# Two feed-forward networks of a hybrid block on one core: pairs of feature tiles by seven half-size products in place of eight

## What is computed

```python
def swiglu(u, w_gate, w_up, w_down):
    return (jax.nn.silu(u @ w_gate) * (u @ w_up)) @ w_down
# u: (528 or 512 tokens, 1024); w_gate, w_up: (1024, 2816); w_down: (2816, 1024)
h = h + 0.5 * swiglu(rmsnorm_2(h, gain), w_gate, w_up, w_down)
```

## Times and profile before

| | us |
|---|---|
| median of three runs (1994.71 to 1995.18) | 1994.72 |
| span of the profiled execution | 1993.0 |
| TensorE busy | 1977.9 |
| GpSimd busy | 939.8 |
| VectorE busy | 870.8 |
| ScalarE busy | 743.8 |

### The profile page before, as it was taken

The page is one execution under the profiler, slowest core; times in us unless marked ns, Lnnn a source line. Parts: engine busy times, 40 slices in busy tenths (PEclk is TensorE's granted clock), DMA queues, the critical chain, the costliest instruction groups (busy, mean ns, idle before and its releaser), DMA issues.

```text
span 1993.0 us, 30195 instructions
## 1 busy us (share of the span) xinstructions
PE 1977.9 (99%) x11350; PEld 1694.2 (85%) x11350; DVE 870.8 (44%) x1516; ACT 743.8 (37%) x1132; POOL 939.8 (47%) x1220
## 2 busy tenths in 40 slices
PE   9999999999999999999999999999999999999998
PEld 6788777899999998789998888888888888888887
DVE  7854776722222225985442253433343542222212
ACT  5733555522222225534443252423334332222321
POOL 6432211654445555453333445354545665554554
PEclk9999999999999999999999999999999999999999
DMA  5211101222222333222111313122322222222322
GB/s 198 78 64 54 43 33 33 85 95 95 90 89 92 99 98 104 74 96 74 64 64 52 115 64 99 66 91 74 101 74 83 93 89 95 95 95 95 104 99 83
DMA packets 49882, 168.68 MB, mean 85 GB/s; under 512 B 6400, under 2 KB 8576, under 8 KB 49792
## 3 DMA queue, kind: packets, MB, share of 16 engines
q1 hardware_dynamic: 46864, 161.89, 24.4%
q10 hardware_dynamic: 2928, 5.51, 0.8%
HBM read 165.29 MB, written 2.10 MB: 84 GB/s over the span
## 4 chain that ended last, share of the span: by engine, by line
PE 94%; DVE 4%; ACT 1%; issue 0%; DMA 0%; DVEq 0%; ACTq 0%
PE slot L2133 93%; DVE qkv L1475 1%; DVE x_lo L1897 0%; PE slot L2588 0%; DVE xt L1889 0%; PE slot L2318 0%; DVE qkv L1472 0%; PE slot L2283 0%; DVE slot L1469 0%; DMA small<-small_in 0%; ACT mixed_hi L966 0%; DVE xt L1428 0%; PE slot L2586 0%; ACT rs L881 0%; DVE x_lo L1435 0%
## 5 line engine op out<-in xcount | busy, mean ns | idle before, releaser
L2666 POOL TENSOR_TENSOR w_lo<-w_raw,w_hi 128x256 fp32r<-128x256 f32 x1216 | 939.6, 805 | 1043.0 <-ACT w_hi L844 784.3
L2133 PE MATMUL slot<-x_hi,w_hi 128*128 128x264 f32 (+1 forms) x1864 | 640.7, 344 | 0.9 <-DVE x_lo L1897 0.7
L2133 PE MATMUL slot<-x_hi,w_lo 128*128 128x264 f32 (+1 forms) x1864 | 629.2, 338 | 0.0
L2133 PE MATMUL slot<-x_lo,w_hi 128*128 128x264 f32 (+1 forms) x1864 | 627.6, 337 | 0.0
L2133 PEld LDWEIGHTS slot<-x_hi,w_hi 128*128 128x128 f32 x1864 | 350.7, 188 | 48.2 <-issue 7.6
L2133 PEld LDWEIGHTS slot<-x_hi,w_lo 128*128 128x128 f32 x1864 | 350.8, 188 | 38.1 <-issue 1.4
L2133 PEld LDWEIGHTS slot<-x_lo,w_hi 128*128 128x128 f32 x1864 | 350.0, 188 | 38.8
L844 ACT ACTIVATE w_hi<-w_raw 128x1024 fp32r<-128x1024 f32 x215 | 225.4, 1054 | 313.8 <-PE slot L2133 305.8
L2133 PE MATMUL slot<-f_hi,w_hi 128*128 128x264 f32 (+2 forms) x550 | 173.5, 316 | 0.0
L2133 PE MATMUL slot<-f_hi,w_lo 128*128 128x264 f32 (+2 forms) x550 | 173.3, 315 | 0.0
L2133 PE MATMUL slot<-f_lo,w_hi 128*128 128x264 f32 (+2 forms) x550 | 172.9, 314 | 0.0
(11 more groups left out here) (366 smaller groups left out, 2863.5 us busy)
## 6 DMA issues: line engine op xcount, KB each, us to landing
w_raw<-weights SPq DMA_DIRECT2D x303, 512.0 KB, 3.2
h<-x_t ACTq DMA_DIRECT2D x4, 512.0 KB, 6.3
dec<-decays ACTq DMA_DIRECT2D x4, 264.0 KB, 3.1
const<-consts SPq DMA_DIRECT2D x1, 576.0 KB, 6.4
at_rot<-rotations ACTq DMA_DIRECT2D x1, 528.0 KB, 4.7
ix_rot<-rotations ACTq DMA_DIRECT2D x1, 528.0 KB, 6.7
rt_rot<-rotations ACTq DMA_DIRECT2D x1, 528.0 KB, 3.8
w_raw<-weights SPq DMA_DIRECT2D x2, 256.0 KB, 4.2
```

The lines of the kernel that those rows point to most:

```text
L2133: return nc.tensor.matmul(out, lhsT, rhs, start=start, stop=stop)
L2666: nc.gpsimd.tensor_tensor(w_lo[j][:, piece], w_raw[j][:, piece], w_hi[j][:, piece].bitcast(F32), ALU.subtract).then_inc(s_lo, 1)
```

## The change

The two feature tiles of a job and the two halves of the tokens make a 2 x 2 block product. It is done by Strassen's scheme in Winograd's form: seven products of 128 x (4 x 128) blocks by half the columns. With A11 to A22 the weight blocks (input tiles are taken in pairs, so `turned` reorders the stream: even tiles, then odd) and B11 to B22 the token blocks, the stationary operands are A11, S1 = A21 + A22, S2 = S1 - A11, A12, S3 = A11 - A21, S4 = A12 - S2 and A22; the moving ones are B11, B12 and B21 (together "B2"), B22, T1 = B12 - B11, T3 = B22 - B12, T2 = T3 + B11 and T4 = B21 - T2.

Each operand has its own high and low part, single-buffered, in places of 512 columns: VectorE makes the four sums of a job one job ahead (`sums`), ScalarE rounds each of the seven when the product of the job before has used its place (`operand_high`), GpSimd makes the low part in one instruction of 512 columns (`operand_low`). The products accumulate in four half-used banks (`pa`, `pe`, `pb`, `pc`; two sets, alternating by job). P2 goes on top of P1; `pb` is seeded by ScalarE with P1 and takes P6, then P3; `pc` is seeded with `pb` and takes P7, then P4. VectorE adds the rest (`evac_job`).

`down` has the same form over rounds of 4 pairs of inner tiles: after gate pairs 4 and 8 come four jobs each that add a round to `h`. The last 6 inner tiles are done as before at the end, for each model tile one weight block and 6 x 3 matmuls (twice that in network 1). The last model tile in network 2 has two column parts still, of 18 matmuls each. In the stages before the networks, `add_to_h` makes the T operands too (`x_parts`) and, at tile 4, the first job's sums. The loops of the engines are written out in place of the hardware loops.

```diff
+def ffn_jobs():
+    jobs = []
+    for p in range(KF // 2):
+        jobs.append(("gate", p))
+        if p and p % ROUND == 0:
+            jobs += [("down", p // ROUND - 1, d) for d in range(KD // 2)]
+        jobs.append(("up", p))
+    return jobs
+ROUND = 4
+ROUNDS = KF // 2 // ROUND
+REST = KF - 2 * ROUND * ROUNDS
+JOBS = ffn_jobs()
+PRODUCTS = ["P1", "P5", "P6", "P2", "P7", "P3", "P4"]
+OPERANDS = ["A11", "S1", "S2", "A12", "S3", "S4", "A22"]
+SUMS = ["S1", "S3", "S2", "S4"]
+BANKS = ["pa", "pe", "pb", "pc"]
+X_PARTS = ["B11", "T1", "T2", "B2", "T3", "T4"]
+X_MADE = ["B11", "T1", "B2", "T3", "T2", "T4"]
+F_PARTS = ["B11", "B2", "T"]
+OPS_OF_FFN = len(X_PARTS) * KD // 2 + len(F_PARTS) * ROUND * ROUNDS + REST
...
+def operand_place(i, name):
+    o = OPERANDS.index(name)
+    return (FFN_FIRST[i] + o // 2) % RING, slice(o % 2 * 512, o % 2 * 512 + 512)
...
+                    sp.wait_ge(s_flo, operand_at(i, n, "A22" if second else "A12"))
+                    sp.wait_ge(s_sum, sum_at(i, n, "S4"))
+                sp.dma_start(w_raw[j][:], w_dram[b // RING, j]).then_inc(s_raw[j], 16)
...
+            def operand_high(i, n, name):
+                j, cols = operand_place(i, name)
+                if n:
+                    act.wait_ge(s_prod, product_at(i, n - 1, PRODUCTS[OPERANDS.index(name)]))
+                else:
+                    act.wait_ge(s_used, whole(FFN_FIRST[i] - RING) + OPERANDS.index(name) // 2 + 1)
+                if name in SUMS:
+                    act.wait_ge(s_sum, sum_at(i, n, name))
+                else:
+                    wait_raw(act, FFN_FIRST[i] + 2 * n + (name[1] == "2"))
+                nc.scalar.activation(w_hi[j][:, cols], weight_part(i, n, name), ACT.Copy).then_inc(s_fhi, 1)
...
+                for n, (kind, p) in enumerate((job[0], job[1]) for job in JOBS):
+                    before = JOBS[n - 1] if n else ("", 0)
+                    nxt = n + 1 < len(JOBS)
+                    if n:
+                        operand_high(i, n, "A22")
+                    else:
+                        operand_high(i, 0, "A22")
+                    for taken in FREE["pb", i, n]:
+                        wait_evac(act, taken)
+                    copy_on(slot(("pb", i, n))[:, 0:half], "pa", "P1", n, 3 * job_at(i, n))
+                    if n == 0:
+                        token_parts(i, KD - 1, width, ("T2", "B2"))
+                    if nxt:
+                        operand_high(i, n + 1, "A11")
+                    act.wait_ge(s_prod, product_at(i, n, "P5"))
+                    if n:
+                        wait_evac(act, ("pb", i, n - 1))
+                    nc.scalar.activation(p5[:, 0:half], slot(("pe", i, n))[:, 0:half], ACT.Copy).then_inc(evac_at(("pe", i, n))[0], 1)
+                    if n == 0:
+                        token_parts(i, KD - 1, width, ("T3", "T4"))
+                        if i == 1:
+                            residual_square(KD - 1)
+                    if nxt:
+                        operand_high(i, n + 1, "S1")
+                    if before[0] == "gate":
+                        for j in range(2):
+                            act.wait_ge(s_q, gates(i, before[1]) + j + 1)
+                            nc.scalar.activation(square[j][:, 0:width], square[j][:, 0:width], ACT.Silu).then_inc(s_fsilu, 1)
+                    for taken in FREE["pc", i, n]:
+                        wait_evac(act, taken)
+                    copy_on(slot(("pc", i, n))[:, 0:half], "pb", "P6", n, 3 * job_at(i, n))
+                    if nxt:
+                        operand_high(i, n + 1, "S2")
+                        operand_high(i, n + 1, "A12")
+                    if before[0] == "up":
+                        ffn_parts(i, before[1], width, ("B11", "B2", 0, 1))
+                    copy_on(u3[:, 0:half], "pc", "P7", n, 3 * job_at(i, n))
+                    if before[0] == "up":
+                        ffn_parts(i, before[1], width, ("T",))
+                    if n == 0:
+                        rsqrt(("norm", 2 * i - 1), 1.0 / D, width)
+                        made["table"] = None
+                    if nxt:
+                        operand_high(i, n + 1, "S3")
+                        operand_high(i, n + 1, "S4")
...
+            def sums(i, n):
+                b = FFN_FIRST[i] + 2 * n
+                wait_raw(dve, b)
+                wait_raw(dve, b + 1)
+                part = lambda name: weight_part(i, n, name)
+                for name, x, y, op in (("S1", "A21", "A22", ALU.add), ("S3", "A11", "A21", ALU.subtract),
+                                       ("S2", "S1", "A11", ALU.subtract), ("S4", "A12", "S2", ALU.subtract)):
+                    if job_at(i, n):
+                        dve.wait_ge(s_flo, len(OPERANDS) * (job_at(i, n) - 1) + OPERANDS.index(name) + 1)
+                    if name in ("S2", "S4"):
+                        dve.wait_ge(s_sum, sum_at(i, n, "S1" if name == "S2" else "S2"))
+                    V.sig(nc.vector.tensor_tensor(part(name), part(x), part(y), op), s_sum, sum_at(i, n, name))
...
+                x_parts(i, j, w)
+                if j == 4:
+                    sums(i, 0)
...
+                def ffn_product(p):
                     for j in range(2):
...
+                        dve.wait_ge(s_fsilu, (i - 1) * KF + 2 * p + j + 1)
+                        V.sig(nc.vector.tensor_tensor(xt[j][:, 0:width], xt[j][:, 0:width], square[j][:, 0:width], ALU.mult),
+                              s_opraw, f_part(i, p, j if p >= ROUND * ROUNDS else F_PARTS[j]))
+                    if p >= ROUND * ROUNDS:
+                        return
+                    raw = fo_raw[:, p % ROUND, :, 0:half]
+                    b11, b12 = xt[0][:, 0:half], xt[0][:, half:width]
+                    b21, b22 = xt[1][:, 0:half], xt[1][:, half:width]
+                    V.sync()
+                    V.own(nc.vector.tensor_tensor(raw[:, 3], b12, b11, ALU.subtract))
+                    V.own(nc.vector.tensor_tensor(raw[:, 5], b22, b12, ALU.subtract))
+                    V.sync()
+                    V.own(nc.vector.tensor_tensor(raw[:, 4], raw[:, 5], b11, ALU.add))
+                    V.sync()
+                    V.sig(nc.vector.tensor_tensor(raw[:, 6], b21, raw[:, 4], ALU.subtract), s_opraw, f_part(i, p, "T"))
+                def ffn_low(p):
+                    if p >= ROUND * ROUNDS:
+                        for j in range(2):
+                            f = 2 * (p - ROUND * ROUNDS) + j
+                            part_low(f_lo[:, f, 0:width], xt[j][:, 0:width], f_hi[:, f, 0:width], f_part(i, p, j))
+                        return
+                    hi, lo = (x[:, p % ROUND, :, 0:half] for x in (fo_hi, fo_lo))
+                    part_low(lo[:, 0], xt[0][:, 0:half], hi[:, 0], f_part(i, p, "B11"))
+                    part_low(lo[:, 1:3], halves(xt[1][:, 0:width]), hi[:, 1:3], f_part(i, p, "B2"))
...
+                def evac_job(n, kind, d, late):
+                    pa, pb, pc = ((bank, i, n) for bank in ("pa", "pb", "pc"))
+                    ps = lambda key: slot(key)[:, 0:half]
+                    if kind == "down":
+                        o11, o12, o21, o22 = (h[:, 2 * d + a, c0 + c * half:c0 + c * half + half] for a in range(2) for c in range(2))
+                        t12, t22 = (x[:, 0:half] for x in xt)
+                    else:
+                        dst = square if kind == "gate" else xt
+                        o11, o12, o21, o22 = (dst[a][:, c * half:c * half + half] for a in range(2) for c in range(2))
+                        t12, t22 = o12, o22
+                    n1, n2 = norm[:, 0:half], norm[:, half:width]
+                    def final(ins_out, src, scale):
+                        if kind == "down":
+                            return nc.vector.scalar_tensor_tensor(ins_out, src, 0.5, ins_out, ALU.mult, ALU.add)
+                        return nc.vector.tensor_tensor(ins_out, src, scale, ALU.mult)
+                    dve.wait_ge(s_prod, product_at(i, n, "P2"))
+                    V.sig(final(o11, ps(pa), n1), *evac_at(pa))
+                    dve.wait_ge(s_seed, 3 * job_at(i, n) + 3)
+                    V.own(nc.vector.tensor_tensor(t22, u3[:, 0:half], p5[:, 0:half], ALU.add))
+                    V.sync()
+                    V.own(final(o22, t22, n2))
+                    late()
+                    dve.wait_ge(s_prod, product_at(i, n, "P3"))
+                    V.sig(nc.vector.tensor_tensor(t12, ps(pb), p5[:, 0:half], ALU.add), *evac_at(pb))
+                    V.sync()
+                    if kind == "gate":
+                        V.sig(final(o12, t12, n2), s_q, (i - 1) * KF + 2 * d + 1)
+                    else:
+                        V.own(final(o12, t12, n2))
+                    dve.wait_ge(s_prod, product_at(i, n, "P4"))
+                    V.sig(final(o21, ps(pc), n1), *evac_at(pc))
+                    V.sync()
+                    if kind == "gate":
+                        dve.sem_inc(s_q, 1)
```

(74 more changed lines are left out.)

412 lines of the change are left out of this document (229 added, 183 removed).

## The result

The changed kernel takes 2136.49 us (median of four runs, 2135.5 to 2140.44) beside 1994.72 of the kernel before on the same chip: a ratio of 1.0714, 95% interval 1.0699 to 1.0729. The change costs 142 us. The forecast was +80, in a range up to 2140. So the direction was right and the size some 60 us short. The profiled execution has a span of 2135.4 us, against 1993.0.

What follows compares the result with a forecast made beforehand. The prediction took TensorE to bound the kernel before and time shared by VectorE and GpSimd the changed one: 1993 + 67 (networks) + 14 (edges) = 2074, plus 1.7, rounded to 2075 us; range 2000 to 2140.

Steps and rivals of the forecast that it cites:

- What bounds the kernel before: Whole kernel before the change: TensorE is the bound, busy for 99% of the span at full clock.
- TensorE's gain: Both networks: fewer or narrower matmuls save 43.6 and 34.8 us, together 78 us, if TensorE stays the bound.
- the pitch: Networks' matmuls: 0.121 us for 264 columns, 0.118 for 256, 0.231 for 512, weight loads included.
- rival 2: Networks: time shared by VectorE and GpSimd on SBUF access decides, on the slow side; 2074 us, chance 72%.
- the floor of 25.3 us a pair: Gate/up pair, network 1: shared time of GpSimd, 15.1 us, plus VectorE's two-SBUF columns, 10.2 us.
- The 4.5%: Networks: lengthening of the shared-time floors, 26.5 us for a network 1 pair, beside a stretch 87 to 100% filled.
- The edges: Network entries, exit and kernel end: VectorE lags and lost overlap, sum 18 us, taken as 14 (4 to 25).
- The term of 8 us for this entry: Entry of network 1: VectorE no longer catches up in the stage before, so the first product waits 8 us.
- Costed at nothing: Jobs: bank-seeding copies, ScalarE's wait loop and DMA lie covered; 10 to 20 us in all if a cover goes.
- its loop of 5.6 us: Each job: ScalarE's wait for VectorE's use of p5, then high parts, silu and P7's seed, stays under a job.
- Rival 1: Networks: TensorE stays the bound, VectorE's instructions falling into GpSimd's gaps; 1925 us, chance 12%.
- Rival 3: Networks: order decides on top, VectorE idling while it has work; 2178 us at most, 2140 half way, chance 12%.

Runs made afterwards that it cites:

- steps in PSUM: Changed kernel with three VectorE evacuation instructions a job written back to and read from PSUM, leaving one SBUF operand instead of two; 2101.82 us, ratio 1.0535.
- narrow sums: Changed kernel with VectorE's four weight sums cut from 512 to 16 columns from each network's second job on, output wrong; 2045.25 us, ratio 1.0253.
- GpSimd in two: Changed kernel with GpSimd making each low part in two instructions of 256 columns instead of one of 512; 2133.05 us, ratio 1.0688.

## Why the prediction was right, and where it was short

**What bounds the kernel before, TensorE's gain, the pitch.** Right. With hardly any low parts 463 matmuls in 56.00 us are 0.121 each and a job of network 1 is 10.2 us, so the half-width products cost what was predicted from the earlier trace rows.

**Direction and mechanism.** Right: rival 2, the shared time of VectorE and GpSimd, decides. The kernel without most low parts is 2.1% faster than the kernel before, with half of them 0.3% faster, and with all of them 7% slower. Three operands a job moved to PSUM give 35 us back. A GpSimd instruction of 512 columns that nothing disturbed took 1.28 us, between the 1.25 and the 1.31 of the prediction. The row that carried this was the one of four pieces in 3.94 us instead of 2.81. The Trainium skill, "SBUF — State Buffer", section "SBUF: two separate sides", describes the port pair as an exclusive lock held for a whole instruction: the sixteen-column sum of 1.17 us agrees. I had cited that rule and then costed it by the column; for the sum that was near enough.

**The step that failed: how full the shared time can be.** The prediction took the floor of 25.3 us a pair 4.5% longer, for 26.5. Measured against the same floor, each with its own load:

| kernel | floor of the shared time, us | pair, us | above |
|---|---|---|---|
| changed | 15.1 + 10.2 = 25.3 | 28.1 | 2.8 |
| steps in PSUM | 15.1 + 8.5 = 23.6 | 26.8 | 3.2 |
| narrow sums | 15.1 + 6.0 = 21.1 | 24.5 | 3.4 |
| GpSimd in two | 25.3 | 27.7 | 2.4 |

(1584 columns fewer in the second, 3968 in the third, at 1.06 ns.) The floor's differences fit within 0.6 us; the amount above it is 2.4 to 3.4 us in these pairs, not 1.2. On 16 early pairs and six late ones those 1.6 us of 28.1 are some 35 of the 60 us that the forecast was short; most of the rest is edges. The 4.5% came from a stretch of twenty microseconds in which GpSimd had nothing to wait for the earlier trace rows. In a pair it has something to wait for. Timelines of GpSimd, ScalarE and VectorE, changed kernel, 456 to 469 us:

```profile
459.45 1.72 POOL L2965 TENSOR_TENSOR w_lo<-w_raw,w_hi 128x512 fp32r<-128x512 f32 x1
465.20 3.81 POOL L2965 TENSOR_TENSOR w_lo<-weight_sum,w_hi 128x512 fp32r<-128x512 f32 x2 [4.03 <-ACT w_hi L1011]
...
461.77 0.64 ACT L1016 ACTIVATE f_ops_hi<-xt 128x528 fp32r<-128x528 f32 x1 [1.26 <-DVE xt L2001]
462.32 0.37 ACT L1061 ACTIVATE u<-slot 128x264 f32<-128x264 f32 x1
463.52 1.09 ACT L1016 ACTIVATE f_ops_hi<-f_ops 128x1056 fp32r<-128x1056 f32 x1 [0.82 <-DVE f_ops L2014]
464.51 1.13 ACT L1011 ACTIVATE w_hi<-weight_sum 128x512 fp32r<-128x512 f32 x2
...
458.29 3.45 DVE L2001 TENSOR_TENSOR xt<-xt,square 128x528 f32<-128x528 f32 x2
```

VectorE's two products wait for GpSimd (3.45 us instead of 1.42); ScalarE waits for them with its token parts; the next high part of a weight stands behind these; and so GpSimd has nothing to do for 4.03 us, while VectorE goes on alone, with the differences and lows that the groups above show at their price alone. The account of a pair is then this. VectorE is full, so the pair is its own 15.9 us plus what it waits: the groups' durations over two pairs sum to 56.3 us for a stretch of 56.2 (neighbours overlap a little), which leaves 12.2 us of waits a pair. GpSimd's exclusive time is 15.1 by the prediction's count. So only some 3 us of GpSimd's work ran beside VectorE's own work that needs no shared access, of which there are 15.9 - 10.2 = 5.7 us. The floor had all 5.7 of them cover GpSimd. What they covered less is the 2.8 us; GpSimd was without work for part of that time. With shorter GpSimd instructions the same chain has GpSimd as its full link. A run that removes only GpSimd's gaps, by placing ScalarE's high parts of weights ahead of its token parts, was not made, so this division is argued from the rows, not shown.

**The edges.** Taken at 14 us. They are 34 with hardly any collision in the networks, and more with all of it: the first job of network 1 waits 8.71 us for a token part whose VectorE work had fallen behind, TensorE's row of the changed kernel:

```profile
394.86 0.59 PE L2425 MATMUL slot<-x_ops_hi,w_hi 128*128 128x264 f32 x1 [8.71 <-DVE x_ops_lo L1924]
```

The term of 8 us for this entry was about half of what came, and the last tiles of network 1 leave VectorE 4.18 us apart (a tile starts at 828.93, the next at 833.11), where the prediction had 3.8. Timeline of VectorE, changed kernel, one such tile:

```profile
828.93 0.69 DVE L2101 SCALAR_TENSOR_TENSOR h<-slot,h 128x528 f32<-128x528 f32 x1
829.65 1.21 DVE L2104 TENSOR_TENSOR square<-h 128x528 f32<-128x528 f32 x1
830.90 1.13 DVE L2109 TENSOR_TENSOR square<-square 128x528 f32<-128x528 f32 x1
831.95 1.24 DVE L2118 SCALAR_TENSOR_TENSOR x_lo<-h,small,x_hi 128x528 fp32r<-128x528 f32 x1
```

The square of `h`, which reads one SBUF tensor as both operands, was costed at 0.71 and took 1.21. The last `x_lo` starts 7 us after TensorE is done, 2.4 in the kernel before.

**Costed at nothing.** The cover that was named is gone: TensorE waits up to 5.3 us for the copy of `pc`. The prediction had 10 to 20 us if a cover goes (its loop of 5.6 us names two high parts and counts one, which makes it 6.2, still under a job). By the three pairs of runs that differ in the copy's place alone it costs 2 to 4 us, since VectorE decides anyway. So a price of nothing was nearly right, for another reason than the one given.

**The rivals.** Rival 1 fell. Rival 3, at 2140 half way, came nearest to the time by its price; half way from 2074 to its 2178 is in fact 2126. By the prediction's own sign, GpSimd with gaps while TensorE waits, it would also be the case to take. But its mechanism is not what the rows show: it had VectorE idle with work at hand, and VectorE is busy for 95%, waits for the shared access included, while moving the copy changes 2 us. The sign was badly chosen, since it does not part the two cases. What is true of rival 3 is the part about GpSimd: it does wait for high parts that stand behind token parts, and that share of the excess is the one that no run isolates. I had asked which engine would be full and not whether both could be at once.

**The signs.** Right: weight sums well over 0.69, GpSimd's 512 columns at 1.6 on average, down jobs near 11 us. Wrong: pairs near 26.5, GpSimd without gaps, TensorE's waits short and released by `w_lo`, the clock full.

**What stays open.** Down jobs alone went from 11.6 and 11.1 us to 10.2 in several of these kernels. A version with the seven products only in `down` was not tried. It would keep the token operands of gate and up off VectorE, and 16 jobs give at most some 20 us.

## What to carry to other kernels

Fewer matmuls are bought with operands that other engines must make; before counting the gain, sum what these instructions hold of an access that two engines share. Such a sum is a floor, and where the two also wait for each other through a third engine they don't reach it: here by some 3 us of 28. If an operand can be had from PSUM, take it from there; three a job were worth 35 us here.

## What the runs showed of the hardware

A VectorE instruction of 16 columns with two SBUF operands took 0.18 us between two GpSimd instructions and 1.17 beside one of 512 columns; instructions of 264 columns with a PSUM operand kept their 0.42 to 0.44 us in full company.

The granted clock was 0.88 over the two pairs and 0.66 from 460 to 470 us. After a gap of 4.30 us TensorE's matmuls started 0.22 us apart, where 0.121 is their pitch at full clock. From 463 to 466 us the granted clock is 0.50, the lower of its two levels, 1.2 in place of 2.4 GHz:

```profile
462.84 0.56 PE L2425 MATMUL slot<-x_ops_hi,w_hi 128*128 128x264 f32 x1 [4.30 <-ACT u L1061]
...
463.41 0.43 PE L2425 MATMUL slot<-x_ops_lo,w_hi 128*128 128x264 f32 x1
463.63 0.43 PE L2425 MATMUL slot<-x_ops_hi,w_hi 128*128 128x264 f32 x1
```

So TensorE, the bound at full clock in the kernel before, works slower here after being made to wait. Since VectorE was full all the while, no run here tells what that cost.
